# Hybrid attention and expert step on one core: the second row block of gathered rows turned with 80 rows for every expert, and scattered with 80 for the last one

## The chip, the cores and the metric

The kernel is one program on 1 core of a Trainium2 chip. The metric is the device time of one execution in microseconds (us); lower is better. The kernel of before has a median of 1916.29 us over 3 runs.

## What is computed

One inference step of a two-layer backbone with shared weights, for 128 context tokens and 512 latent tokens of width 1024, all in fp32. Each layer has a modulated RMSNorm, a mixer (differential attention beside a short convolution), a second RMSNorm and a SwiGLU channel mixer. The first layer's mixer is dense. The second layer's picks 2 of 8 experts for each token, and that is where the change lies:

```python
def moe_swiglu(h, w_router, w_gu, w_down):
    logits = (t @ w_router).astype(jnp.float32)
    top_v, top_i = lax.top_k(logits, TOP_K)
    top_w = jax.nn.softmax(top_v, axis=-1)
    gates = jnp.einsum('nk,nke->ne', top_w, jax.nn.one_hot(top_i, N_EXPERTS, ...))
    g, u = jnp.split(jnp.einsum('nd,edf->enf', t, w_gu), 2, axis=-1)
    eo = jnp.einsum('enf,efd->end', jax.nn.silu(g) * u, w_down)
    y = jnp.einsum('ne,end->nd', gates, eo)
```

The result is scaled by a gate, added to the residual stream, and normalized once more.

## The kernel before

**Engines and number format.** Tokens are columns, features are partitions, in most stages. Every fp32 weight tile of 128 x 1024 (a chunk) is loaded by the SP queue into one of 6 buffers `raw` (L604), rounded by ACT to `w_hi` (L1383), and DVE forms the rest `w_lo` (L1943), in 3 buffers. TensorE (PE) multiplies hi by hi, hi by lo and lo by hi. PSUM is one tensor `ps` of 4 slots, each of two banks of 512 columns. PE waits in `open_block` for a slot, and DVE frees slots by `blk_free`.

**The experts.** Where no expert has more than 208 tokens the kernel computes only the chosen rows. The experts are sorted by load. `ROOM` (L29) is the number of slots for each: 208, 192, 184, 176, 168, 160, 160, 160. Each expert's rows lie in two row blocks: the first has 128 rows, the second the rest. `NROWS` (L30) is `[128, ROOM - 128]` for each expert: second blocks of 80, 64, 56, 48, 40, 32, 32, 32 rows. `ROWS` (L28) is `[128, 80]`, the largest.

**Order of work.** `main_items` (L89) writes the order out by hand, and `main_plan` (L109) numbers the steps and gives each its PSUM slot. All engines follow the same list in `main_expert`. For each expert e it is: 22 chunks up (`gu`), then the two `tr` steps of expert e+1, then 11 chunks down (`down`). A chunk's split for two steps later is queued on ACT and DVE at the head of each step.

**Turning the rows.** GpSimd gathers the rows of an expert's tokens from memory into `gx` (L1829), `NROWS[e]` rows of each block, well ahead. A `tr` step (L1253 to L1261) transposes four feature blocks of `gx` into a PSUM slot, for each the first row block (128 rows) and then the second (`NROWS[e][1]` rows), so two steps make 16 transposes per expert. The pieces of feature block k lie at column `(k % 2) * ROOM[e]`, the second at 128 beyond. ACT copies the slot to `hg` (L1620) and DVE forms the low part (L2450), `2 * ROOM[e]` columns of each bank.

**The last expert.** The outputs of experts 0 to 6 go through memory and are joined to the residual `x_tok` while the last expert runs. The last one stays on the chip. For each half of 512 features and both row blocks DVE scales `ey` (L2485), ACT rounds it to `ey_hi` (L1631), and DVE makes `ey_lo` (L2495), `NROWS[7]` rows each, 128 and 32. PE then scatters the rows to the tokens by the selection `selT`. For tokens of tiles 0 and 1 the sum starts from `x_tok` (`seed`, L1195) and `scatter_on` (L1204) adds four matmuls for each half, waiting for each operand. They go in the order hi of block 0, hi of block 1, lo of block 0, lo of block 1. For tiles 2 to 4 `scatter` (L1131) does four matmuls for each half without waits, in the order hi and lo of block 0, hi and lo of block 1.

**The end.** For each tile of 128 tokens: DVE adds the scatter to `x_tok` (L2503, tiles 2 to 4), ACT squares and sums (L1653) and takes the root (L1656), DVE the reciprocal (L2521). ACT scales the row (L1636), or GpSimd for tiles 2 and 3 (L1898). PE turns it back (`turn_tokens`, L1220, with one dummy product L1214 before most). DVE (L2528) and ACT (L1804) multiply by the last gain, and SP stores ten blocks of 256 KB (L695).

Of the kernel before, what the change touches and what calls it, by code (L numbers as in the profile page):

```python
# [263 lines left out]
def hybrid_step(nc, xT, condT, ada_w, in_w, out_w, gu_w, down_w, router_w, b_ada, g_mix, g_ffn, g_fin, lam_qk,  # L264
                subln, conv_w, kcT, vc, cos, sin, ident, iota, below, moe_down_w, y, newk, newv):
    with ExitStack() as ctx:
# [494 lines left out]
        def _(pe):  # L761
# [115 lines left out]
            for l in range(LAYERS):  # L877
# [193 lines left out]
                else:  # L1071
# [51 lines left out]
                                     start=True, stop=True).then_inc(mm_done, 1)  # L1123
                    tile_rows(7, 4)

                    def scatter(g, t, hf, u, nrows=ROWS):

                        for st_ in range(ST):
                            rows = slice(0, nrows[st_])
                            for part in (ey_hi, ey_lo):  # L1130
                                ins = nc.tensor.matmul(ps[:, g % 4, hf, :], selT[rows, u, st_, t * P:(t + 1) * P],  # L1131
                                                       part[rows, st_, hf * 512:(hf + 1) * 512],
                                                       start=(st_ == 0 and part is ey_hi),
                                                       stop=(st_ == ST - 1 and part is ey_lo))
                        return ins
# [62 lines left out]
                    def scatter_on(g, t, hf, hi_count):  # L1198

                        for part, ready in ((ey_hi, ahi_done), (ey_lo, alo_done)):  # L1200
                            for st_ in range(ST):
                                rows = slice(0, NROWS[LAST_E][st_])
                                pe.wait_ge(ready, hi_count + st_ + 1)
                                ins = nc.tensor.matmul(ps[:, g % 4, hf, :], selT[rows, 1, st_, t * P:(t + 1) * P],  # L1204
                                                       part[rows, st_, hf * 512:(hf + 1) * 512], start=False,
                                                       stop=(st_ == ST - 1 and part is ey_lo))
                        return ins
# [22 lines left out]
                    def main_expert(part):  # L1230
                        oo = operand[l, "act"]
                        for kind, e, i, q, g, c in part:
# [11 lines left out]
                            if kind == "idx":  # L1244
                                fill(g0 + g + 1, FILL["ranks"])
                                pe.wait_ge(sel_ready, 1)
                                pe.wait_ge(tok_ready, 1)
                                for st_ in range(ST):
                                    for t in range(TT):
                                        ins = nc.tensor.matmul(ps[0:ROWS[st_], slot, st_, 0:2],  # L1250
                                                               sel[:, t, st_ * P:st_ * P + ROWS[st_]], tok[:, t, :],
                                                               start=(t == 0), stop=(t == TT - 1))
                            elif kind == "tr":  # L1253
                                if i == 0:
                                    pe.wait_ge(gx_in, 16 * ST * (e + 1))
                                for k in range(4):
                                    for st_ in range(ST):
                                        at, some = (k % 2) * ROOM[e] + st_ * P, NROWS[e][st_]
                                        ins = nc.tensor.transpose(ps[:, slot, k // 2, at:at + some],  # L1259
                                                                  gx[0:some, st_, (4 * i + k) * P:(4 * i + k + 1) * P],  # L1260
                                                                  idn[0:some, 0:some])  # L1261
                            elif kind == "gu":
                                if i == 0:
                                    if e == 0:
                                        fill(g0 + g, FILL["rows"])
                                    pe.wait_ge(alo_done, oo + LO_BASE[e] + 2)
                                ins = up_chunk(n0 + c, ps[:, slot, 0, 0:ROOM[e]], ps[:, slot, 0, 0:2 * ROOM[e]],
                                               gathered_rows(e))
                            elif kind == "turn":
                                pe.wait_ge(gates_ready, 1)  # L1270
                                pe.wait_ge(sel_ready, 2)
                                ins = turn_slots(slot, i, glast)
                            elif kind == "xt":
                                ins = turn_stream(slot, i)
                            else:
                                pe.wait_ge(alo_done, oo + LO_BASE[e] + 2 + i + 1)
                                if e == 0:
                                    ins = down_chunk(n0 + c, g0 + g, i)
                                elif (e, i) == (LAST_E, FB - 1):

                                    down_upper(n0 + c, g0 + g, i).then_inc(upper_done, 1)
                                    ins = down_lower(n0 + c, g0 + g, i)
                                else:
                                    down_lower(n0 + c, g0 + g, i)
                                    ins = down_upper(n0 + c, g0 + g, i)
# [67 lines left out]
                    with pe.Else():  # L1353
# [9 lines left out]
                        for t, hf in LAST_ORDER:  # L1363
                            if t in SEEDED:
                                scatter_on(lg + t, t, hf, last_lo - ST * (2 - hf)).then_inc(mm_done, 1)
                                if (t, hf) == (0, 0):
                                    seed(lg + 1, 1, 1)
                                continue
                            if hf == 0:
                                open_block(lg + t)  # L1370
                            scatter(lg + t, t, hf, 1, NROWS[LAST_E]).then_inc(mm_done, 1)
                        turn_tokens(lg + TT, POOLED, 1)


# [1 line left out]
        def _(act):  # L1376
# [75 lines left out]
            for l in range(LAYERS):  # L1452
# [142 lines left out]
                else:  # L1595
# [29 lines left out]
                    def last_outputs_hi():  # L1625
                        for hf in range(2):
                            for st_ in range(ST):

                                rows, cols = slice(0, NROWS[LAST_E][st_]), slice(512 * hf, 512 * (hf + 1))
                                act.wait_ge(ey_scaled, ST * hf + st_ + 1)  # L1630
                                nc.scalar.activation(ey_hi[rows, st_, cols], ey[rows, st_, cols], ACT.Copy)\  # L1631
                                    .then_inc(ahi_done, 1)
# [299 lines left out]
        def _(dve):  # L1932
# [138 lines left out]
            for l in range(LAYERS):  # L2071
# [246 lines left out]
                else:  # L2318
# [158 lines left out]
                    def last_outputs(g, done0):  # L2477
# [3 lines left out]
                        for hf in range(2):  # L2481
                            cols = slice(512 * hf, 512 * (hf + 1))
                            for st_ in range(ST):
                                rows = slice(0, NROWS[LAST_E][st_])
                                nc.vector.scalar_tensor_tensor(  # L2485
                                    ey[rows, st_, cols], ey[rows, 1, cols] if st_ else ps[rows, g % 4, hf, :],
                                    gslot[rows, 1, st_:st_ + 1],
# [2 lines left out]
                                dve.wait_ge(ey_scaled, 2 * ST)  # L2490
                                dve.sem_inc(blk_free, ST)
                            for st_ in range(ST):
                                rows = slice(0, NROWS[LAST_E][st_])
                                dve.wait_ge(ahi_done, done0 + ST * hf + st_ + 1)
                                nc.vector.tensor_tensor(ey_lo[rows, st_, cols], ey[rows, st_, cols],  # L2495
                                                        ey_hi[rows, st_, cols].bitcast(F32), ALU.subtract)\
# [375 lines left out]
```

## Time and profile before

| | |
|---|---|
| median of 3 runs | 1916.29 us (1916.16 to 1916.88) |
| the profiled execution | 1912.51 us |
| its span on the core | 1910.7 us |
| mean granted TensorE clock | 0.985 |
| PE, DVE, ACT, GpSimd busy | 97%, 58%, 41%, 7% of the span |
| expert stage, first turned row to last down matmul | about 1231.7 to 1872.3 us |
| from there to the end | 38.4 us |

The profile is one execution. PE is the matmul side of TensorE, PEld its weight loads, which run beside the matmuls; a transpose is recorded as one load and one matmul. A shape such as `32*128 32x32` reads: 32 active rows and 128 active columns of the array, operand of 32 partitions by 32 elements. Starts of matmuls are recorded, their ends are modelled, so the distance from start to start tells the pace, and "busy" does not show gaps between pipelined instructions. "Idle ... <-issue" is time in which an engine waited for nothing that the profile shows. The granted clock is the share of TensorE's full 2.4 GHz that it was allowed.

### The profile page before, as it was taken

The page shows a single profiled execution, that of the slowest core. Times are in us where ns is not written, and L with a number is a line of the kernel's source. Part 1 is how long each engine was busy: PE and PEld are TensorE (multiplying, and loading weights), DVE is VectorE, ACT ScalarE, POOL GpSimd, SP SyncE. Part 2 cuts the span into 40 slices and gives each one's busy share as a digit, 9 for nine tenths or more (in the row PEclk, how much of TensorE's full clock was granted, in tenths as well). Part 3 has the DMA queues.
Part 4 walks back from the last instruction along what each step waited for, and adds up shares of the span by engine and source line. Part 5 has one row for each costly group of instructions (what it writes and reads, how often), then busy time and mean ns, then how long its engine had stood idle before and what let it go on. Part 6 is the DMA issues. An engine that isn't in the chain of part 4 may idle for free.

```text
span 1910.7 us, 30889 instructions
## 1 busy us (share of the span) xinstructions
PE 1844.9 (97%) x12347; PEld 1690.1 (88%) x12347; DVE 1115.5 (58%) x1907; ACT 790.8 (41%) x1335; POOL 142.7 (7%) x109
## 2 busy tenths in 40 slices
PE   7999989999999999999999899699999999999988
PEld 6999867999999999999998579697998989989875
DVE  2653786453432344447437862575776867768685
ACT  4221264422221222232222643364655656656564
POOL 2000000200000000020000001330000000002211
PEclk8999999999999999999999999799999999999997
DMA  9425100323332242223363000596787877878861
GB/s 359 171 101 221 56 1 12 122 100 140 115 100 78 100 179 86 78 89 142 123 191 86 1 15 9 157 233 206 226 285 218 266 234 241 272 223 328 271 192 56
DMA packets 93847, 290.56 MB, mean 152 GB/s; under 512 B 15368, under 2 KB 23944, under 8 KB 93696
## 3 DMA queue, kind: packets, MB, share of 16 engines
q1 hardware_dynamic: 86784, 271.20, 43.4%
q0 software_dynamic: 6912, 17.30, 2.7%
q8 instruction: 101, 1.65, 0.4%
q14 instruction: 50, 0.41, 0.1%
HBM read 281.98 MB, written 12.28 MB: 154 GB/s over the span
## 4 chain that ended last, share of the span: by engine, by line
PE 88%; DVE 5%; issue 2%; ACT 2%; DMA 1%; POOL 0%; SPq 0%; ACTq 0%; DVEq 0%; POOLq 0%
PE ps L776 48%; PE ps L1144 11%; PE ps L1167 6%; PE ps L1145 5%; PE ps L1177 4%; PE ps L842 2%; PE ps L971 2%; PE ps L917 2%; PE ps L1155 2%; PE ps L1148 2%; PE ps L1259 1%; DVE nbias L2099 1%; PE ps L1147 1%; DVE pr L2116 1%; PE ps L1131 1%
## 5 line engine op out<-in xcount | busy, mean ns | idle before, releaser
L1943 DVE TENSOR_TENSOR w_lo<-raw,w_hi 128x1024 fp32r<-128x1024 f32 x394 | 482.6, 1225 | 354.8 <-ACT w_hi L1383 345.4
L1383 ACT ACTIVATE w_hi<-raw 128x1024 fp32r<-128x1024 f32 x394 | 414.5, 1053 | 320.8 <-PE ps L776 171.1
L1144 PE MATMUL ps<-hg,w_hi 128*128 128x320 f32 (+5 forms) x1232 | 348.0, 352 | 6.3 <-DVE w_lo L1943 4.0
L776 PE MATMUL ps<-a_hi,w_hi 128*128 128x320 f32 x1472 | 341.4, 313 | 3.4 <-DVE a_lo L1974 3.4
L776 PE MATMUL ps<-a_hi,w_lo 128*128 128x320 f32 x1472 | 336.5, 310 | 0.0
L776 PE MATMUL ps<-a_lo,w_hi 128*128 128x320 f32 x1472 | 333.4, 307 | 0.0
L1145 PE MATMUL ps<-hg,w_lo 128*128 128x160 f32 (+5 forms) x1232 | 301.5, 245 | 0.0
L776 PEld LDWEIGHTS ps<-a_hi,w_hi 128*128 128x128 f32 x1472 | 247.0, 188 | 12.1 <-issue 8.1
L776 PEld LDWEIGHTS ps<-a_lo,w_hi 128*128 128x128 f32 x1472 | 248.4, 188 | 0.0
L776 PEld LDWEIGHTS ps<-a_hi,w_lo 128*128 128x128 f32 x1472 | 245.0, 188 | 0.0
L1144 PEld LDWEIGHTS ps<-hg,w_hi 128*128 128x128 f32 x1232 | 233.6, 190 | 7.9 <-DVE w_lo L1943 4.5
L1145 PEld LDWEIGHTS ps<-hg,w_lo 128*128 128x128 f32 x1232 | 236.7, 192 | 0.4
L1991 DVE TENSOR_REDUCE bcol<-ps 128x2 f32<-128x4 f32 x84 | 13.5, 160 | 184.9 <-PE ps L776 184.8
L1167 PE MATMUL ps<-w_hi,ea 128*128 128x512 f32 x308 | 85.9, 401 | 3.6 <-DVE w_lo L1943 3.6
L776 PE MATMUL ps<-act_hi,w_hi 128*128 128x320 f32 x352 | 80.3, 309 | 0.0
L776 PE MATMUL ps<-act_hi,w_lo 128*128 128x320 f32 x352 | 80.3, 309 | 0.0
L776 PE MATMUL ps<-act_lo,w_hi 128*128 128x320 f32 x352 | 80.3, 309 | 0.0
L1911 POOL COPY ss<-sq 128x640 f32<-128x640 f32 x4 | 3.3, 822 | 1022.9 <-ACT sq L1394 1022.9
L917 PE MATMUL ps<-kT,qT 64*128 64x512 f32 (+2 forms) x288 | 63.4, 486 | 11.9 <-ACT pr L1501 11.9
L1594 ACT ACTIVATE act_hi<-tt 128x640 fp32r<-128x640 f32 x22 | 16.3, 740 | 140.9 <-DVE tt L2000 140.9
L1501 ACT ACTIVATE pr<-ps,nbias 128x768 f32<-128x768 f32 (+1 forms) x80 | 63.5, 794 | 26.6 <-DVE nbias L2099 15.3
L1167 PEld LDWEIGHTS ps<-w_hi,ea 128*128 128x128 f32 x308 | 57.6, 189 | 17.4 <-DVE w_lo L1943 4.3
(321 smaller groups left out, 2633.7 us busy)
## 6 DMA issues: line engine op xcount, KB each, us to landing
raw<-gu_w SPq DMA_DIRECT2D x220, 512.0 KB
raw<-moe_down_w SPq DMA_DIRECT2D x88, 512.0 KB
ada_raw<-ada_w SPq DMA_DIRECT2D x21, 2048.0 KB, 8.1
raw<-in_w SPq DMA_DIRECT2D x48, 512.0 KB
raw<-down_w SPq DMA_DIRECT2D x22, 512.0 KB
raw<-out_w SPq DMA_DIRECT2D x16, 512.0 KB
ada_pro<-ada_w SPq DMA_DIRECT2D x2, 2048.0 KB, 18.9
y_rows<-ey POOLq DMA_DIRECT2D x7, 512.0 KB
```

The costliest lines, as they stand in the source:

```text
L776: ins = nc.tensor.matmul(out[:, hf, 0:c1 - c0], w, o[:, c0:c1], start=f, stop=e)
L842: ins = nc.tensor.matmul(ps[32 * j:32 * (j + 1), g % 4, 0, 0:QCOLS], cs[:, QUAD * q + k, :], src[:, k, j * QCOLS:(j + 1) * QCOLS], start=f ...
L917: ins = nc.tensor.matmul(score_rows(l, m)[:, c0:c1], qT[rows, h, t * P:(t + 1) * P], kT[rows, h, k0 + c0:k0 + c1], start=True, stop=True)
L971: ins = nc.tensor.matmul(outputs(l)[:, i % 2, :], pT[:, i % 2, j * P:(j + 1) * P], vtok[:, k0 // P + j, h * VH:(h + 1) * VH], start=(j == ...
L1144: nc.tensor.matmul(sums, whi, both, start=(k == 0), stop=False)
L1145: nc.tensor.matmul(out, wlo, rows_[:, k, 0, :], start=False, stop=False)
L1148: ins = nc.tensor.matmul(sums, whi, both, start=False, stop=True)
L1167: ins = nc.tensor.matmul(ps[:, g % 4, hf, :], ea[:, k, LOWER * a:LOWER * a + P], w[:, n % SPLIT, hf * 512:(hf + 1) * 512], start=(k == 0 a ...
L1177: ins = nc.tensor.matmul(ps[:, (g + 1) % 4, hf, :], ea[:, k, P:2 * P], w[:, n % SPLIT, hf * 512:(hf + 1) * 512], start=(k == 0 and w is w_ ...
L1383: nc.scalar.activation(w_hi[:, s, :], raw[:, n % RAW, :], ACT.Copy).then_inc(hi_done, 1)
L1501: nc.scalar.activation(pr[:, i % 2, s, 0:nk], score_rows(l, m)[:, 0:nk], ACT.Exp, bias=nbias[:, m % 4:m % 4 + 1], accum_out=rsum[:, STEPS[ ...
L1943: nc.vector.tensor_tensor(w_lo[:, s, :], raw[:, n % RAW, :], w_hi[:, s, :].bitcast(F32), ALU.subtract)\
```

## The change

Everywhere that `NROWS` limited the second row block on PE or in the last expert's operands, `ROWS` takes its place: 80 rows for every expert. The gather (L1828) and the copies of outputs (L2656, L2667, L1734) keep `NROWS`. The rows of `gx` above those gathered hold what an earlier expert left there; their columns in PSUM are overwritten by the next transpose or lie outside what is copied. In the scatter the added slots have zeros in `selT`.

```diff
@@ scatter, and its call for the last expert
-                    def scatter(g, t, hf, u, nrows=ROWS):
+                    def scatter(g, t, hf, u):
-                            rows = slice(0, nrows[st_])
+                            rows = slice(0, ROWS[st_])
...
-                            scatter(lg + t, t, hf, 1, NROWS[LAST_E]).then_inc(mm_done, 1)
+                            scatter(lg + t, t, hf, 1).then_inc(mm_done, 1)
@@ scatter_on
-                                rows = slice(0, NROWS[LAST_E][st_])
+                                rows = slice(0, ROWS[st_])
@@ main_expert on PE, kind == "tr"
-                                        at, some = (k % 2) * ROOM[e] + st_ * P, NROWS[e][st_]
+                                        at, some = (k % 2) * ROOM[e] + st_ * P, ROWS[st_]
@@ last_outputs_hi on ACT
-                                rows, cols = slice(0, NROWS[LAST_E][st_]), slice(512 * hf, 512 * (hf + 1))
+                                rows, cols = slice(0, ROWS[st_]), slice(512 * hf, 512 * (hf + 1))
@@ last_outputs on DVE, at L2484 and at L2493
-                                rows = slice(0, NROWS[LAST_E][st_])
+                                rows = slice(0, ROWS[st_])
```

## Rows read from the trace of the kernel before

**Rows 1.** The page, part 1 (PE) and part 4 (chain that ended last).
```profile
PE 1844.9 (97%) x12347; PEld 1690.1 (88%) x12347; DVE 1115.5 (58%) x1907; ACT 790.8 (41%) x1335; POOL 142.7 (7%) x109
...
PE 88%; DVE 5%; issue 2%; ACT 2%; DMA 1%; POOL 0%; SPq 0%; ACTq 0%; DVEq 0%; POOLq 0%
```

**Rows 2.** Timeline of PE, expert 0's transposes: start us, us, engine, line, operands, count.
```profile
1232.32 1.16 PE L1259 MATMUL ps<-idn,gx 80*128 80x80 f32 x11
1233.32 0.31 PE L809 MATMUL ps<-ones 128*128 128x128 f32 x1
```

**Rows 3.** Stretches, L1259 alone: us, PE busy, PEld busy, clock, DMA share, GB/s.
```profile
1291.97:1295.60 3.63, 3.63 (x16) 2.04 (x15) 1.00 0.72 244
...
1532.92:1536.40 3.48, 3.48 (x16) 2.05 (x15) 1.00 0.83 247
...
1762.39:1765.80 3.41, 3.41 (x16) 2.05 (x16) 1.00 0.98 315
```

**Rows 4.** Groups by shape, L1259's weight loads: busy, mean ns | idle before.
```profile
L1259 PEld LDWEIGHTS ps<-idn,gx 32*128 32x128 f32 x24 | 3.2, 134 | 3.1 <-issue 0.6
...
L1259 PEld LDWEIGHTS ps<-idn,gx 80*128 80x128 f32 x7 | 1.0, 142 | 0.0
```

**Rows 5.** Timeline of PE, the last down chunks (eight starts between the two).
```profile
1868.62 0.63 PE L1167 MATMUL ps<-w_lo,ea 128*128 128x512 f32 x2
...
1870.49 0.63 PE L1177 MATMUL ps<-w_lo,ea 128*128 128x512 f32 x2
```

**Rows 6.** The chain that ended last, in order of time: start us, us, what.
```profile
1878.46 4.94 PE ps L1204 x12
1883.40 13.32 PE ps L1131 x24
```

**Rows 7.** Stretches of the tail: PE, PEld, DVE, ACT, POOL busy, clock, DMA.
```profile
1882.00:1884.00 2.00, 2.00 (x6) 0.84 (x5) 0.16 (x1) 1.70 (x4) 0.00 (x0) 0.98 0.00 0
1886.00:1890.00 4.00, 4.00 (x8) 1.74 (x8) 1.39 (x2) 1.15 (x3) 0.00 (x0) 0.50 0.00 0
1894.00:1898.00 4.00, 4.00 (x12) 2.35 (x12) 1.22 (x1) 0.86 (x3) 2.54 (x1) 0.50 0.00 0
1898.00:1902.00 4.00, 4.00 (x25) 4.00 (x25) 2.82 (x6) 2.60 (x4) 2.84 (x1) 0.63 0.41 118
```

**Rows 8.** Timeline of DVE beside expert 7's transposes.
```profile
1763.26 0.31 DVE L2629 TENSOR_TENSOR tt<-tt,ps 128x160 f32<-128x160 f32 x1
...
1767.61 1.23 DVE L1943 TENSOR_TENSOR w_lo<-raw,w_hi 128x1024 fp32r<-128x1024 f32 x1
```

**Rows 9.** Groups by shape on DVE, the last expert's scaling: busy, mean ns.
```profile
L2485 DVE SCALAR_TENSOR_TENSOR ey<-ps,gslot,x 128x512 f32<-128x512 f32 x2 | 1.5, 740 | 0.0
L2485 DVE SCALAR_TENSOR_TENSOR ey<-ey,gslot,x 32x512 f32<-32x512 f32 x2 | 1.5, 730 | 0.0
```

**Rows 10.** Timeline of the end on DVE, ACT and POOL.
```profile
1896.76 1.22 DVE L2503 TENSOR_TENSOR x_tok<-x_tok,ps 128x1024 f32<-128x1024 f32 x1 [3.18 <-PE ps L1131]
1898.02 1.06 ACT L1653 ACTIVATE yab<-x_tok 128x1024 f32<-128x1024 f32 x1 [3.12 <-DVE x_tok L2503]
1898.13 0.16 DVE L2521 RECIPROCAL trms<-trms 128x1 f32<-128x1 f32 x1
1898.38 2.84 POOL L1898 TENSOR_SCALAR yab<-x_tok,trms 128x1024 f32<-128x1024 f32 x1 [1.84 <-DVE trms L2521]
...
1900.29 1.15 ACT L1636 ACTIVATE yab<-x_tok,trms 128x1024 f32<-128x1024 f32 x1 [0.80 <-DVE trms L2521]
1903.16 2.24 ACT L1804 ACTIVATE x<-ps,gfin 128x128 f32<-128x128 f32 x8 [1.72 <-PE ps L1220]
```

**Rows 11.** Timeline of PE, one up chunk's first matmul and the next one's.
```profile
1758.27 0.31 PE L1144 MATMUL ps<-hg,w_hi 128*128 128x320 f32 x1
1758.42 0.23 PE L1145 MATMUL ps<-hg,w_lo 128*128 128x160 f32 x1
...
1760.33 0.31 PE L1144 MATMUL ps<-hg,w_hi 128*128 128x320 f32 x1
```

More of the change, by code:

```diff
@@ L2492, in last_outputs @@
                             for st_ in range(ST):
-                                rows = slice(0, NROWS[LAST_E][st_])
+                                rows = slice(0, ROWS[st_])
                                 dve.wait_ge(ahi_done, done0 + ST * hf + st_ + 1)
```

## Prediction

> **What bounds the kernel now.** I read the page's busy times and its chain first, then the timeline of TensorE (PE) where the diff touches it, then the weight loads' idle time, then the granted clock. PE is busy for 97% of the span and carries 88% of the chain that ended last [rows 1], so a microsecond taken off PE's own stream in the expert stage should come off the time, as long as ACT and DVE, which split the weights for it, keep up. "Busy" is no proof of useful work, though, and the timeline shows where. The sixteen transposes of expert 0 (second block 80 rows) run at 11 starts in 1.00 us, 0.091 us each [rows 2]. The same sixteen of experts 1 to 7 (second block 64, 56, 48, 40, 32, 32, 32 rows) take 3.63 us down to 3.41 us, 0.21 to 0.23 us each, at the full granted clock ([rows 3] hold experts 1, 4 and 7 of the seven). They move fewer columns and take over twice as long. The weight loads say why: of the 32-row loads each has about 0.13 us of idle before it (3.1 us over 24), while the 80-row loads of expert 0 have none [rows 4]. So a load for the full array is fetched ahead behind the running transpose, and one that changes from 128 rows to 64 or fewer, or back, waits until the array is empty. Expert 0 alternates 128 and 80 rows and pays nothing: 80 is on the side of 128.
>
> The Trainium skill fits these rows: its page "TensorEngine Tiling (Array Packing)", Key Properties, says that changing the tiling mode drains TensorE, and its Tiling Modes are 128, 64 or 32 rows; by that rule 80 rows need the undivided array, and the trace agrees ([rows 2, 3]).
>
> The last scatter has the same pattern, 128 rows and 32 rows in turn. A 128x512 matmul of the last down chunks starts every 0.234 us (8 in 1.87 us) [rows 5]. The seeded scatter (L1204) needs 4.94 us for 12, 0.41 each, and the plain one (L1131) 13.32 us for 24, 0.555 each [rows 6]. The second figure has another part: the granted clock is 1.00 until shortly before 1884, 0.50 from there to 1898, and is on its way back within 1898 to 1902 [rows 7]. That is 1.2 in place of 2.4 GHz. Before it fell PE had no idle time by the records, but it was streaming 512 columns only half of the time, half of them with 32 rows; it rose in the transposes that follow, all 128 rows and dense.
>
> **The change, part by part.**
>
> *Turned rows.* Seven experts have 16 transposes each, 8 of them widened to 80 rows. Today: 3.63 + 3.59 + 3.53 + 3.48 + 3.42 + 3.42 + 3.41 = 24.48 us [rows 3]. After: 7 x 16 x 0.091 = 10.2 us [rows 2]. That is 14.3 us less, the added columns included, because expert 0 already moves 80. The bounds: 14.3 less where the gap is wholly a matter of row count, and 1.8 more where it is not (rivals, below). I take the first, because expert 0 is the same line, tiles and queue.
>
> *What hides behind it.* Behind each block stand the down chunks of the expert before. They need the last up block out of PSUM (DVE L2629, ends 1763.57 for expert 7) and later w_lo of the third chunk (starts 1767.61, ends 1768.84) [rows 8]. PE comes to the first at 1762.39 + 1.46 = 1763.85, 0.3 us after it is free. It comes to the third chunk at 1763.85 + 20 x 0.234 = 1768.5. That is before 1768.84, but this split stands in ACT's and DVE's queues behind the second copy of the turned rows, which waits for PE today; with the turn 1.9 us earlier, the two copies run back to back and w_lo ends near 1768.0. What is late next is thus just in time; I give back 0.3 us over all seven blocks, with 0 and 7 us (1 us each) as ends.
>
> *Nothing else moves there.* The gathers still bring 64 to 32 rows; rows above stay what an earlier expert left and fall outside what is used. No DMA, wait or queue entry is added or moved. The copies out of PSUM keep their sizes.
>
> *Last expert on ACT and DVE.* Four copies and eight DVE operations go from 32 to 80 partitions at the same 512 columns. The 32-partition form takes 730 ns, the 128-partition one 740 [rows 9]: 0.1 us in all, taken as 0.
>
> *Seeded scatter.* The first four of its matmuls wait for ey_hi and ey_lo, as now. The other 12: 4.94 us today, 12 x 0.234 = 2.8 after [rows 5, 6]: 2.1 us less. No row shows waits of this kind without a change of rows; if the wait before each matmul also keeps its load back, the gain is 0. I take 2.1, since the idle time before the loads of [rows 4] comes with the row change alone, with no wait between those transposes.
>
> *Plain scatter.* 24 x 0.234 = 5.6 us at the full clock, against 13.32: 7.7 us less [rows 5, 6]. I take the full clock: the engine now has neither 32-row matmuls nor empty stretches, and the down chunks before, dense and of 128 rows, run at 2.4 GHz (512 columns are 0.213 us there, the start distance 0.234). At the low clock it is 24 x 0.47 = 11.2, only 2.1 less.
>
> *What is late next at the end.* The tail has a second chain: per token a DVE add of 1.22, ACT square 1.06 and two small steps (1.7 in all with the handoffs, an estimate), reciprocal 0.16, scaling about 1.1; for tokens 2 and 3 the scaling is on GpSimd at 2.84 [rows 10]. Run forward with these, in times that leave the turned rows' gain out: PE ends the seeded scatter near 1881.1, token 2 at 1882.9, token 3 at 1884.8, token 4 at 1886.6. ACT begins token 0 near 1880.3 and has it scaled at 1884.4; token 2, added by 1884.2, is squared and rooted by 1885.9, and only then token 1 is scaled, by 1886.9. That frees PSUM for the transposes, 0.3 us after PE is through. GpSimd scales token 2 from 1886.2 to 1889.1 and token 3 to 1892.0; the transposes of tokens 3 and 4, 1.1 us each, follow to 1894.3. Today they run to about 1904.2: the last ACT copies, which wait for them, end at 1905.40 [rows 10]. So the end comes 9.9 us earlier, and the stores behind it (the last ACT copy ends at 1905.40, the span at 1910.7) have a little more room. I take 10.0.
>
> **Sum.** 14.3 - 0.3 + 10.0 = 24.0 us. The profiled execution took 1912.51 us with a span of 1910.7, so 1.8 lie around it; it would be 1888.5. The median of the runs is 1916.29, 3.8 above the profiled one, and I keep that distance: **1892 us**.
>
> **Rivals.**
>
> 1. *The low clock stays in the scatter.* For it: the fall in the present tail starts right after the seeded scatter, whose waits on ACT and DVE remain. Against: [rows 7] show the full clock still in 1882 to 1884, more than 3 us into its last twelve matmuls, and those now come closer together. Gain 14.0 + 2.1 + 2.1 = 18.2: 1898. Chance 0.13.
> 2. *Waits take the place.* At each block the down chunks wait for w_lo or PSUM after all, 1 us per block; the tail gains. 24 - 7 = 17: 1899. For it: the 0.3 us of slack. Against: order and lengths of the copies. Chance 0.06.
> 3. *Only columns count.* The gap is something else than the rows, such as what happens to run beside experts 1 to 7. From 64 to 32 rows a block loses 0.22 us for 256 columns, 0.86 ns a column [rows 3]; the change adds 8 x (16+24+32+40+3x48) = 2048 columns: +1.8 us; the scatter keeps its 512 columns and changes by nothing: 1918. Against it: the pace is uniform in seven blocks, and the idle time goes with the row change [rows 4]. Chance 0.06. The Trainium skill's page "TensorE: Matmul & The Clock Gate", Step-by-step, says of a weight load that its time scales with the columns and that the row count does not matter: by it alone nothing would be gained; the loads' own lengths agree (134 ns at 32 rows, 142 at 80), the idle before them does not.
> 4. *Slower: writes in PSUM wait for each other.* The widened transpose writes columns 128 to 207, and the next one begins at column 192 to 160, over its last 16 to 48. That is 4 places per expert, 28 in all. If today's distances are waits for a former write to the same bank, they stay, and each overlap adds up to another 0.21 us: 28 x 0.21 + 1.8 = 7.7: 1924. With the distances kept, 0.07 us per place makes it slower by over 0.2%; were they gone, 0.9 us would be needed. Against it: the sixteen matmuls of an up chunk, 1758.27 to 1760.33, all write the same columns and start 0.13 us apart (2.06 us over 16), while they last 0.23 to 0.31 us and more [rows 11]. Chance 0.05.
>
> That the wider shape is not what runs can be left out: the line takes it from ROWS, as expert 0 does today.
>
> **How the numbers follow.** The likeliest case has 0.70, its own range 1889 to 1895 (distance of the runs to the profile, 0 to 3 us of waits, up to 2 us of the seeded scatter, 1 us of stores). The range to 1900 takes in rivals 1 and 2, and 1888 allows the stores to end sooner. Rivals 3 and 4 are left out, with 0.11. A measurement of this kernel tells some 0.2%, 3.8 us, from no change. Faster: 0.70 + 0.13 + 0.06 = 0.89; within 0.2%: rival 3, 0.06; slower: rival 4, 0.05.
>
> **What would show it.** Turned rows: seven blocks of 16 transposes near 1.5 us each, no idle before the 80-row loads. If PE's first down matmul is followed by idle with w_lo or PSUM named, rival 2 holds. Tail: L1131 in about 5.6 us at clock 1.00; near 11 at 0.50 is rival 1. GpSimd's second scaling should become the releaser of a wait on PE. Blocks of 3.5 us with 80 rows mean that rivals 3 or 4 hold and my reading of the gap is wrong; above 5 us it is rival 4.

## The result, and the profile after

| | before | after |
|---|---|---|
| median | 1916.59 us (4 runs, 1916.16 to 1920.43) | 1885.99 us (4 runs, 1884.07 to 1886.11) |
| profiled execution | 1912.51 us | 1886.11 us |
| its span | 1910.7 us | 1884.3 us |
| mean granted clock in it | 0.985 | 0.990 |

The ratio is 0.9839, 95% interval 0.982 to 0.9858 (27.2 to 34.5 us): 30.6 us faster by the medians, 26.4 us by the two profiled spans. The forecast was 1892 with a range of 1888 to 1900, so the kernel came out below the range.

The page of after, parts 1 and 4, against [rows 1]:

```profile
PE 1818.4 (97%) x12347; PEld 1680.9 (89%) x12347; DVE 1115.4 (59%) x1907; ACT 789.5 (42%) x1335; POOL 141.1 (7%) x109
...
PE 87%; DVE 6%; issue 2%; DMA 2%; ACT 2%; POOL 1%; SPq 0%; POOLq 0%; ACTq 0%; DVEq 0%
```

PE has the same 12347 instructions and is 26.5 us less busy. Its share stays at 97%: this was never idle time by the records, but matmuls that stood behind each other.

Stretches of the turned rows in after, L1259 alone (columns as in [rows 3]), and the groups of its weight loads by shape between 1286 and 1800 us, which answer to [rows 4]:

```profile
1290.18:1291.61 1.43, 1.43 (x16) 1.43 (x15) 1.00 0.74 264
1525.00:1526.43 1.43, 1.43 (x16) 1.43 (x15) 1.00 0.81 255
1748.56:1750.06 1.50, 1.50 (x16) 1.44 (x16) 1.00 0.99 366
```

```profile
L1259 PEld LDWEIGHTS ps<-idn,gx 80*128 80x128 f32 x56 | 8.0, 142 | 0.1
L1259 PEld LDWEIGHTS ps<-idn,gx 128*128 128x128 f32 x56 | 7.9, 142 | 0.0
```

The seven blocks take 1.43 to 1.54 us each, 10.3 in all where they took 24.4. The idle time before the narrow loads, 3.1 us over 24, is 0.1 over 56. The weight loads themselves became no shorter (142 ns, where the 32-row loads took 134): only the gaps between them went.

The chain that ended last in after, its last pieces in order of time (start us, us, what), which answers to [rows 6]:

```profile
1863.82 1.45 PE ps L1204 x5
1865.26 3.75 PE ps L1131 x16
1869.01 0.02 issue
1869.03 1.23 DVE x_tok L2503
1870.27 0.02 issue
1870.29 0.17 DVE trms L2521
1870.46 0.09 issue
1870.56 2.86 POOL yab L1898
1873.42 2.83 POOLq L266
1876.25 0.04 issue
1876.30 1.11 PE ps L1220 x8
1877.40 0.02 issue
1877.43 1.46 ACT x L1804 x5
```

In before, PE carried this chain alone from the seeded scatter to the last transposes. Now it leaves PE after token tile 2 and runs through GpSimd's two scalings (2.86 and, under POOLq, 2.83 us) back to PE. The timeline of PE has the wait that the prediction asked for:

```profile
1876.30 1.09 PE L1220 MATMUL ps<-idn,yab 128*128 128x128 f32 x8 [1.51 <-POOL yab L1898]
```

The clock in the tail of after (columns as in [rows 7]) stays at 1.00 until PE has done its work:

```profile
1861.00:1863.00 2.00, 2.00 (x8) 1.31 (x7) 1.49 (x3) 1.26 (x2) 0.00 (x0) 1.00 0.00 0
1865.00:1868.00 3.00, 3.00 (x15) 2.43 (x14) 1.00 (x2) 2.94 (x7) 0.00 (x0) 1.00 0.01 3
1868.00:1871.00 3.00, 2.86 (x13) 1.99 (x11) 1.94 (x4) 2.67 (x6) 0.44 (x1) 1.00 0.02 5
```

Read between first starts of PE's lines, the spans differ so:

| stretch | before | after | gained |
|---|---|---|---|
| start to expert 1's block | 1291.97 | 1290.18 | 1.8 |
| the seven blocks | 24.4 | 10.3 | 14.2 |
| between the blocks, and down to the seeded scatter's first start (L1195) | 555.9 | 555.6 | 0.3 |
| L1195 to the plain scatter (L1131) | 10.98 | 9.02 | 2.0 |
| L1131 to the first final transpose (L1220) | 13.32 | 5.91 | 7.4 |
| L1220 to the end | 14.01 | 13.28 | 0.7 |

That is 26.4. (From the first start of L1204, the seeded scatter itself went from 7.93 to 5.80 us, 2.1 gained.) The other 4.2 of the 30.6 is the distance between median and profiled execution: +4.1 before (1916.59 against 1912.51), -0.1 after.

### The profile page after: what moved, and what is told of

Read it like the earlier page. It is cut to its first block, busy times and chain, and to the rows that moved or that the text cites. A ratio compares the mean times of both kernels' runs of the same rounds, so it can differ in the third digit from the quotient of the medians.

```text
span 1884.3 us, 30889 instructions
## 1 busy us (share of the span) xinstructions
PE 1818.4 (97%) x12347; PEld 1680.9 (89%) x12347; DVE 1115.4 (59%) x1907; ACT 789.5 (42%) x1335; POOL 141.1 (7%) x109
## 4 chain that ended last, share of the span: by engine, by line
PE 87%; DVE 6%; issue 2%; DMA 2%; ACT 2%; POOL 1%; SPq 0%; POOLq 0%; ACTq 0%; DVEq 0%
PE ps L776 48%; PE ps L1144 11%; PE ps L1167 5%; PE ps L1145 5%; PE ps L1177 4%; PE ps L842 3%; PE ps L971 2%; PE ps L917 2%; PE ps L1155 2%; PE ps L1148 2%; DVE nbias L2099 1%; PE ps L1147 1%; DVE pr L2116 1%; DVE w_lo L1943 1%; DMA yab<-y_rows,late 1%
## 5 line engine op out<-in xcount | busy, mean ns | idle before, releaser
L1144 PE MATMUL ps<-hg,w_hi 128*128 128x320 f32 (+5 forms) x1232 | 346.8, 351 | 5.0 <-DVE w_lo L1943 3.7
L1144 PEld LDWEIGHTS ps<-hg,w_hi 128*128 128x128 f32 x1232 | 232.9, 189 | 6.6 <-DVE w_lo L1943 4.2
L1167 PE MATMUL ps<-w_hi,ea 128*128 128x512 f32 x308 | 85.8, 401 | 3.7 <-DVE w_lo L1943 3.6
L1167 PEld LDWEIGHTS ps<-w_hi,ea 128*128 128x128 f32 x308 | 57.5, 189 | 17.7 <-DVE w_lo L1943 4.8
```

The costliest lines, as they stand in the source:

```text
L1144: nc.tensor.matmul(sums, whi, both, start=(k == 0), stop=False)
L1167: ins = nc.tensor.matmul(ps[:, g % 4, hf, :], ea[:, k, LOWER * a:LOWER * a + P], w[:, n % SPLIT, hf * 512:(hf + 1) * 512], start=(k == 0 a ...
```

## The experiments

Two things were open: whether the row change is the cause, and where its limit lies; and why the gain by medians is so much above the forecast. All ratios are to the kernel of before, run on the same chip beside them. Times between first starts are used throughout, so that seeded means first start of L1204 to first of L1131, and plain from there to the first of L1220 (before: 7.93 and 13.32; after: 5.80 and 5.91).

### Each part alone

**before_again** is the kernel of before unchanged.

> The kernel before, unchanged. Theory A: the change itself is worth 14.2 us in the turned rows and 10.1 in the tail; the rest of the difference of the medians (30.6 us) is how executions of the same code differ, by how long the low clock lasts around the start of the expert stage (1208 to 1242 us in the trace of before) and in the tail. It expects a median near 1916 here, and spans of single executions that differ by steps of 1.7 us or more, with the mean granted clock going with them; the profile of before was a short one. Rival B: the change also shortens a part outside the turned rows and the tail. It expects every execution here, profiled or not, within 0.5 us of the others in the stages up to the expert stage, and the profiled execution at 1912.5 again.

It has a median of 1915.69 us over 10 runs (1912.38 to 1918.22), ratio 0.9994 (0.998 to 1.0007). Its profile showed what that of before had not. Stretches of before_again over expert 1's block and right behind it (columns as in [rows 7]):

```profile
1290.70:1294.40 3.70, 3.70 (x18) 2.16 (x17) 2.65 (x6) 1.53 (x3) 0.00 (x0) 1.00 0.77 245
1294.40:1298.00 3.60, 3.60 (x11) 2.45 (x12) 2.33 (x3) 1.75 (x2) 0.00 (x0) 0.60 0.04 18
```

The clock falls as the turned rows end, for 3.4 us, here and again at 1380 behind expert 2's block. The stages with these falls are longer than the same stages of before: 86.28 against 84.71 us and 79.93 against 78.45. One fall costs some 1.5 to 1.6 us.

The tail differs too. The clock falls at 1882.2, inside the seeded scatter and 2.7 us before the plain one, and stays low for 20.5 us; in before it fell at 1883.9, just behind the plain one's start, for 17.1 us. The stretch between that fall and the plain scatter, then the two scatters in the chain:

```profile
1882.20:1884.80 2.60, 2.60 (x4) 0.91 (x4) 0.16 (x1) 1.39 (x3) 0.00 (x0) 0.50 0.00 0
```

```profile
1878.91 6.02 PE ps L1204 x12
1884.93 13.80 PE ps L1131 x24
```

So seeded takes 9.00 us and plain 13.80, and from the first start of L1204 to the end it is 36.8 us against 35.3 in before and 25.0 in after.

**turn_only** widens only the transposes:

```diff
-  at, some = (k % 2) * ROOM[e] + st_ * P, NROWS[e][st_]
+  at, some = (k % 2) * ROOM[e] + st_ * P, ROWS[st_]
```

> Only the transposes take 80 rows; the last expert's operands and scatter stay at 32. Theory A: seven blocks at 1.43 to 1.54 us in place of 3.4 to 3.6, the tail as before (10.98 us seeded, 13.32 plain), time 14 us below before: 1902. If the low clock in the tail depends on where the tail falls in time and not on what it does, the tail may be shorter: then 1892 to 1895. Rival that only columns count: 1.8 us above before.

1899.2 us (1894.84 to 1902.54), ratio 0.9903 (0.9874 to 0.9932). The blocks take 1.49 us; the tail is that of before_again (seeded 8.94 us, plain 13.80, at 0.50). By the medians the part is worth 17.7 us against before's 1916.89 beside it, where the blocks give 14.2; the interval (13.0 to 24.2 us) holds both. Behind expert 1's block the stretch of turn_only reads:

```profile
1294.40:1298.00 3.60, 3.60 (x17) 2.68 (x16) 2.81 (x4) 3.26 (x5) 0.00 (x0) 1.00 0.43 139
```

No fall behind any block. The chain:

```profile
1863.93 5.96 PE ps L1204 x12
1869.89 13.80 PE ps L1131 x24
```

**scatter_only** is after with the transposes set back to `NROWS[e][st_]` (the edit of turn_only the other way).

> Only the last expert's operands and scatter take 80 rows; the transposes keep 64 to 32. Theory A: transposes as before at 3.4 to 3.6 us a block; tail 10.1 us shorter, the seeded scatter's matmuls at 0.234 us where operands are there, the plain scatter 5.9 us at clock 1.00; time 1906. Rival: the clock falls here as in before, the plain scatter takes 11 us and the time is 1911.

1906.24 us (1905.15 to 1907.05), ratio 0.994 (0.9917 to 0.9963): worth 10.65 us. Seeded 5.79, plain 5.91 and end 13.27 are those of after to 0.01. The blocks are back at 3.4 to 3.8, and so are falls at their ends, at 1298 and 1462. The expected 1906 came, without the fall in the tail that its rival held possible.

**after_again** is the changed kernel once more.

> The changed kernel, unchanged, on the same chip as the three others. Theory A: 1886, the sum of the two parts within 1 us (before - turn_only plus before - scatter_only equals before - this). Rival B: the sum misses by 2 us or more.

1887.99 us (1886.8 to 1888.36), ratio 0.9844 (0.9822 to 0.9867), 28.9 below before's median; the parts alone sum to 17.7 + 10.65 = 28.3. No interaction shows, though the intervals are some 4 to 6 us to either side.

### Where the limit lies, and whether it is the changes or the width

**turn_64** and **turn_72** give every expert from 1 to 7 the same second row block in the transposes, in the kernel of before:

```diff
-  at, some = (k % 2) * ROOM[e] + st_ * P, NROWS[e][st_]
+  at, some = (k % 2) * ROOM[e] + st_ * P, (P, 64 if e else 80)[st_]
```

turn_72 has 72 in place of 64.

> The kernel before, with 64 rows in place of 56 to 32 in the second block's transposes of experts 2 to 7 (experts 0 and 1 as they are). Theory A (the array is emptied at each change between 128 rows and 64 or fewer): every block of experts 1 to 7 takes the 3.63 us of expert 1, idle before the loads stays, time some 0.9 us above before. Theory C, new after the first runs: behind such a block the granted clock falls to 0.50 for 3.4 us in some executions and costs 1.7 us each time; it expects such falls here as in before. Rival (fewer rows than 80 are slow by degrees): blocks of 2.5 us and less.

> The kernel before, with 72 rows in the transposes of experts 1 to 7. Theory A, by which 65 rows and more use the undivided array: blocks of 1.4 to 1.5 us, no idle before the loads, no fall of the clock behind them, time 1898 as with 80 rows alone (1899.2). Rival by degrees: blocks of 2 us and more.

turn_64: 1913.48 us (1910.2 to 1918.64, 10 runs), ratio 0.9991 (0.9977 to 1.0006), no difference that shows; its profile has the expected blocks, but none of the expected falls of the clock. turn_72: 1896.7 us (1896.33 to 1899.26), ratio 0.9897 (0.9875 to 0.992). A block of expert 5 in turn_64, the same view as [rows 3]:

```profile
1608.71:1612.34 3.63, 3.63 (x16) 2.06 (x16) 1.00 0.83 264
```

and the timeline of PE for expert 7's block in turn_72:

```profile
1748.96 1.58 PE L1259 MATMUL ps<-idn,gx 128*128 128x128 f32 x16
1750.46 0.70 PE L1167 MATMUL ps<-w_hi,ea 128*128 128x512 f32 x2
```

With 64 rows every block takes 3.63 us, with 72 it takes 1.38 to 1.50, with 80 it takes 1.43 to 1.54. The limit lies between 64 and 72 rows, and from 72 to 80 a block grows by some 0.05 us at most. This also explains the slope of [rows 3]: the fall from 3.63 to 3.41 us went with the size of the second row block (rows and columns shrink together in a transpose), since it is gone where the size is the same, and the rest of a block is the same sixteen gaps.

**turn_grouped** keeps the narrow rows of before and swaps the two loops, so that four blocks of 128 rows and then four narrow ones follow each other in each of the two steps: 4 changes of rows per expert in place of 16, and no matmul wider.

```diff
-  for k in range(4):
-      for st_ in range(ST):
+  for st_ in range(ST):
+      for k in range(4):
```

> The kernel before with its 64 to 32 rows, but each tr step transposes the four first row blocks and then the four second ones, so that the row mode changes 4 times per expert and not 16. Theory A (the change of mode costs, some 0.125 to 0.145 us each, not the small transpose): blocks of 1.8 to 2.0 us, time 1902 to 1904. Rival (transposes of 64 rows and fewer are slow in themselves, whatever stands beside them): blocks stay at 3.4 to 3.6, time 1916.

1903.26 us (1899.19 to 1908.66, 6 runs), ratio 0.9936 (0.9916 to 0.9955). The timeline of PE for expert 7's block:

```profile
1751.94 1.91 PE L1259 MATMUL ps<-idn,gx 128*128 128x128 f32 x16
1753.78 0.51 PE L1167 MATMUL ps<-w_hi,ea 128*128 128x512 f32 x1
```

1.84 us from start to start, against 3.41 with the same matmuls in turn: 1.57 us for 12 changes fewer, 0.13 us each. So it is the change of rows that costs, neither the narrow rows nor the columns. The seven blocks take 13.0 us in all; widening to 80 gains a further 2.7. This kernel's scatters are those of before, and slower still in its profile (seeded 12.94, low clock for 30.7 us from 1867), 4 us that go into its longest run, 1908.66; what made the clock fall earlier there is not known.

### The two scatters and the clock

**on_narrow** is after with only the seeded scatter back at 32 rows (`rows = slice(0, NROWS[LAST_E][st_])` at L1202). **plain_narrow** is after with only the plain scatter back (`scatter` takes `nrows` again, as in before):

```diff
-  scatter(lg + t, t, hf, 1).then_inc(mm_done, 1)
+  scatter(lg + t, t, hf, 1, NROWS[LAST_E]).then_inc(mm_done, 1)
```

> The changed kernel, but the seeded scatter (L1204) reads 32 rows of the second block again; the plain scatter keeps 80. Theory C: the seeded part takes 7.9 to 9.0 us again (2 to 3 more), and the clock, which falls for what is done in the seeded part, is at 0.50 as the plain scatter begins; with dense 128- and 80-row matmuls it comes back within the plain scatter, so that one takes 6 to 9 us. Time 1890 to 1893. Rival: the clock stays at 1.00 throughout, because only the plain part with 32 rows pulls it down: plain 5.9 us, 1890.

> The changed kernel, but the plain scatter (L1131) reads 32 rows of the second block again; the seeded one keeps 80. Theory C: the seeded part stays at 5.8 us; the plain one starts at clock 1.00, where its 24 matmuls are 0.335 us apart (8.0 us), and ends at 0.50 if the clock falls in it: 8 to 12 us against 5.9. Time 1889 to 1893. Rival: the clock never falls without the seeded part's gaps: 8.0 us and 1.00 to the end, 1889.

on_narrow: 1889.36 us (1888.6 to 1890.05), ratio 0.9861 (0.9839 to 0.9883); seeded 7.94, plain 6.01. Its chain, then its stretches over the scatter (columns as in [rows 7]):

```profile
1862.65 4.94 PE ps L1204 x12
1867.59 3.94 PE ps L1131 x16
```

```profile
1860.00:1867.00 7.00, 6.85 (x17) 2.87 (x16) 3.51 (x6) 2.53 (x5) 0.00 (x0) 1.00 0.00 1
1867.00:1873.00 6.00, 6.00 (x26) 4.64 (x25) 2.93 (x5) 4.76 (x10) 0.00 (x0) 1.00 0.01 4
```

Theory C expected a fall of the clock here, and it did not come: the narrow seeded scatter alone costs 2.1 us, all of it row changes.

plain_narrow: 1890.73 us (1890.1 to 1892.11), ratio 0.9869 (0.9847 to 0.9892); seeded 5.79, plain 7.82. Its chain and stretches:

```profile
1866.84 7.73 PE ps L1131 x24
```

```profile
1867.00:1874.00 7.00, 7.00 (x23) 3.12 (x22) 2.94 (x5) 5.87 (x11) 0.51 (x1) 1.00 0.02 4
1875.00:1879.00 4.00, 4.00 (x25) 4.00 (x24) 3.06 (x7) 2.40 (x4) 4.00 (x2) 0.62 0.23 64
```

The plain scatter with 32 rows takes 7.82 us at the full clock and 5.91 with 80: 1.9 us of row changes. The clock falls only behind it, for 3.4 us. So of the 7.4 us that plain gained in after, 5.5 (13.32 - 7.82) is clock and 1.9 is row changes, and in these profiles the clock is low in the plain scatter only where both scatters read 32 rows.

**scatter_64** is after with 64 rows in both scatters (`(P, 64)` at both places); ACT and DVE still make 80.

> The changed kernel, but both scatters read 64 rows of the second block: the mode changes as often as with 32, twice the rows are active. Theory A: seeded part 7.9 to 9.0 us, plain part at least 7.8. What lowers the clock in the tail of before is open: if it goes by the gaps that the mode changes leave, the clock falls here too, plain part 13.3 and more, time 1896 or above; if it goes by how many rows are active, it stays at 1.00 or comes back sooner, plain part 7.8 to 10, time 1891 to 1893.

1894.13 us (1889.65 to 1898.41), ratio 0.9893 (0.9863 to 0.9923). Its chain and stretches:

```profile
1865.81 4.95 PE ps L1204 x12
1870.76 5.31 PE ps L1131 x16
```

```profile
1863.00:1870.00 7.00, 6.84 (x17) 2.87 (x16) 3.67 (x6) 2.53 (x5) 0.00 (x0) 1.00 0.00 1
1870.00:1878.00 8.00, 8.00 (x25) 3.48 (x25) 2.94 (x5) 5.99 (x12) 0.38 (x1) 1.00 0.01 3
```

The pace is that of 32 rows (4.95 us for the twelve as in [rows 6]; plain 7.94 against 7.82), so in the scatter too 64 rows pay for the change in full. But the clock stays at 1.00 in this profile, where with 32 rows in both scatters it fell before or at the start of the plain one in all ten profiles that have them (plain 13.32 us in before, 13.80 in the other nine, where the fall came inside the seeded one). The same stretch in before_again:

```profile
1884.00:1898.00 14.00, 14.00 (x25) 6.27 (x25) 2.77 (x4) 6.30 (x11) 2.31 (x1) 0.50 0.01 2
```

It is one profile. The four runs spread over 9 us at mean clocks from 0.984 to 0.990, and their median lies above the 1891 to 1893 expected for a kept clock, so that 64 rows keep the clock in every execution isn't shown.

### What ends the kernel now

The new chain runs through GpSimd's scaling of tiles 2 and 3. **pooled_one** leaves it only tile 2 and gives tile 3 to ACT:

```diff
-SEEDED, POOLED, SHARED = (0, 1), (2, 3), (3, 4)
+SEEDED, POOLED, SHARED = (0, 1), (2,), (3, 4)
```

> The changed kernel with the scaling of token tile 3 on ACT and not on GpSimd, which is the releaser of PE's last wait in the trace of after (two scalings of 2.84 us in a row). Theory: the last transposes start 1.0 us sooner, time 1.0 us below after. Rival: ACT, which has the roots and the other scalings, is late in its place, no difference.

> The changed kernel once more, on the chip of the three others, to compare pooled_one with: 1886 to 1888.

pooled_one: 1887.68 us (1881.41 to 1891.19, 5 runs), ratio 0.9862 (0.9839 to 0.9885). **after_third**, the changed kernel beside it: 1885.37 us (1882.91 to 1889.58, 5 runs), ratio 0.9848 (0.9825 to 0.9872). The gain of 1.0 us did not come: L1220 to the end is 13.27 us in both. ACT ended 1.4 us sooner against the first transposes, but the ten stores had not. The stretch from 1865 to 1880 us in pooled_one, DMA busy tenths in 40 slices, and the stores:

```profile
DMA  1000000000008999999999999999999999995000
...
y<-x SPq DMA_DIRECT2D x10, 256.0 KB, 3.3
```

From the first store to the last the DMA engines are full: 2.62 MB at some 285 GB/s is 9.2 us. So the end goes with the start of the stores and what they take, not with the last scaling. pooled_one's own shortest execution (1881.41) is also the profiled one; its span is shorter ahead of the tail, not in it.

### More profiles of before

The falls behind the blocks could explain the excess of the medians, but the profile on which the forecast was made had none. **before_look1**, **before_look2** and **before_look3** are before unchanged, **turn_look1** is turn_only again, one profiled execution each.

> The kernel before, one more profiled execution. Theory C: in most executions of before the granted clock falls to 0.50 for 3.4 us right behind one to three of the seven blocks of turned rows of experts 1 to 7 (stage between two blocks 1.6 us longer each time). Rival D: the two falls seen in before_again and the two in scatter_only were chance, not tied to the blocks: falls then lie anywhere in the expert stage, or there are none.

> As before_look1: Theory C one to three falls, each right behind a block of turned rows; rival D none or elsewhere.

> As before_look1: Theory C one to three falls, each right behind a block of turned rows; rival D none or elsewhere.

> Only the transposes take 80 rows, one more profiled execution. Theory C: no fall behind any of the seven blocks. Rival D: as many as in before.

1909.68, 1910.54, 1917.84 and 1896.52 us, one run each; the one run of before beside them took 1923.12. The first two and turn_look1 have no fall behind a block. before_look3 has three, behind the blocks of experts 1, 4 and 7 (two stretches of block and what follows, then the third fall; columns as in [rows 7]):

```profile
1292.00:1295.70 3.70, 3.70 (x18) 2.13 (x16) 2.63 (x6) 1.53 (x3) 0.00 (x0) 1.00 0.81 248
1296.20:1299.50 3.30, 3.30 (x10) 2.30 (x9) 2.18 (x2) 1.27 (x2) 0.00 (x0) 0.55 0.01 2
1534.50:1538.00 3.50, 3.50 (x18) 2.09 (x16) 2.68 (x8) 1.29 (x3) 0.00 (x0) 1.00 0.78 247
1538.40:1541.50 3.10, 3.10 (x9) 2.39 (x8) 2.08 (x2) 1.34 (x2) 0.00 (x0) 0.50 0.06 24
1771.00:1773.00 2.00, 2.00 (x6) 1.60 (x5) 1.59 (x2) 1.18 (x2) 0.00 (x0) 0.50 0.71 289
```

Over all profiles of this case:

| turned rows | profiles | blocks | falls right behind a block |
|---|---|---|---|
| 64 to 32 rows, in turn (before, before_again, before_look1 to 3, scatter_only, turn_64) | 7 | 49 | 0, 2, 0, 0, 3, 2, 0: 7 |
| 72 or 80 rows, or grouped (the other eleven) | 11 | 77 | 0 |

Theory C's "in most executions" is not borne out: two of the five profiles of before have such falls. Nor are these the only falls of the stage. From expert 1's block to the seeded scatter the 18 profiles have 23 more, with narrow and with wide blocks alike, and each begins while PE waits 1.6 to 3.4 us for w_lo, or up to 1.8 us after that wait. Such a wait and the fall with it in before, a timeline line and a stretch with columns as in [rows 7]:

```profile
1740.09 0.41 PE L1144 MATMUL ps<-hg,w_hi 128*128 128x320 f32 x1 [2.32 <-DVE w_lo L1943]
```

```profile
1740.60:1744.00 3.40, 3.40 (x16) 3.40 (x16) 3.04 (x6) 1.44 (x5) 2.79 (x3) 0.50 0.69 257
```

The seven of the table have no such wait near them. They begin between 0.8 us before and 0.6 us after the end of a narrow block.

## Why the prediction was right in its mechanism and missed the time

**Turned rows: right.** 14.3 us less was forecast, 14.2 came, with gathers, ACT and DVE left as they were. At each change between 128 rows and 64 or fewer PE loses some 0.13 us; it is shown by changing the rows and nothing else (turn_64 against turn_72) and by changing the order and nothing else (turn_grouped).

**Rival 3 falls, rival 4 falls.** Columns cost some 0.8 ns each (a block of expert 1 takes 1.38 us in turn_72 and 1.43 in after, with 64 columns more), near the 0.86 of [rows 3], but the change did not come out slower. The page "TensorE: Matmul & The Clock Gate" of the Trainium skill, Step-by-step, says that the row count does not matter to a weight load. For the load itself this holds (142 ns at 80 and at 128 rows, 134 at 32). For the pace of matmuls in turn it does not: turn_64 and turn_72 differ by 2.1 to 2.2 us per block. The widened transposes overlap a former one in PSUM at 28 places, and the blocks run at 0.09 us per transpose all the same, so writes to the same bank do not wait for each other here.

**Waits behind the blocks (0.3 us lost, rival 2 with 7): right that they are small.** The stretch between the blocks came out 0.3 us shorter in this pair, but it differs by more between profiles of one kernel (before 552.5 to 558.5 us, after 552.6 to 555.7), so 0.3 either way can't be read from it. That rival 2 is out is shown by the waits: PE's waits of the expert stage in after name w_lo alone, 3.7 us in front of L1144 and 3.6 in front of L1167, two each; before they were 4.0 and 3.6.

**Seeded scatter, 2.1 us: right** for the row changes (2.1 in the first pair, 2.1 in on_narrow). The waits before each of its matmuls do not keep the loads back: where the operands are there, starts are 0.23 to 0.24 us apart. In the four other profiles of before the clock falls inside this scatter, which then takes 8.7 to 9.0 us, so that 2.9 to 3.2 are gained; the sum had no term for that.

**Plain scatter, 7.7 us at the full clock: right** (7.4 measured, 5.91 against 5.6; 7.9 against the 13.80 of the four other profiles). Rival 1, the low clock staying, is dead: in all seven profiles with 80 rows in one scatter or both, the clock is 1.00 through it. The reason given was partly wrong. "Neither 32-row matmuls nor empty stretches" named two things, and scatter_64, with the gaps and without the 32 rows, kept the clock too. By that one profile the active rows counted, not the gaps alone.

**End, in all 10.0 us for the tail: right for this pair** (10.1), with GpSimd's second scaling as the releaser. That it fits so well is in part luck of the profile: from the first start of L1204 to the end, before's first profile took 35.3 us, its four others 36.5 to 36.8, and after 25.0 each time, so 11.5 to 11.8 is what the tail gains in those. That ACT's and DVE's wider operands cost next to nothing holds too: the scaling L2485 of block 1 takes 739 ns with 80 partitions, 730 with 32. But the 0.7 us behind L1220 is bounded by the stores, not by GpSimd, as pooled_one shows.

**The sum against the profiled pair.** It gave 24.0 us, and 26.4 came. Of the difference 1.8 lies ahead of expert 1, where nothing changed. The low clock at the start of the expert stage lasted 20.5 us in before and 17.1 in after, and between 13.7 and 23.9 in other executions of either kernel. That is chance of the execution.

**The step that failed** in the prediction is "the median of the runs is 1916.29, 3.8 above the profiled one, and I keep that distance". It takes the distance for something that lies around both kernels alike. It did not stay: it was 4.1 us before and -0.1 after. Part of it is time that this change takes away, and that the one profile of before, from which every term was read, happened not to have:

- Falls of the clock behind narrow blocks: none in that profile, 0, 2, 0, 0 and 3 in the five of before, so one per execution on the mean, 1.6 us. The sum had no term for the clock there, because the one profile showed 1.00 in all seven blocks.
- The earlier fall in the tail: 1.2 to 1.5 us in the four other profiles, 1.1 on the mean of the five.

With both, the sum is 24.0 + 1.6 + 1.1 = 26.7. By the means of the profiles the stretches that the change touches gain 27.2 us: 14.2 in the blocks, 1.6 in the falls behind them, 11.4 from L1204 to the end. Without the distance kept, the sum as it stood gives 1912.5 - 24.0 = 1888.5, above the 1886.0 that was measured (1888.0 and 1885.4 for the same kernel later).

**What stays open.** These terms narrow the gap and don't close it. 1916.29 less 26.7 is 1889.6, and the medians of after lie 28.9 to 30.6 us below those of before beside them. The means of the whole profiled executions lie 25.0 apart (1913.0 for the five of before, 1888.0 for the three of after), 2.2 less than those 27.2. Of the 2.2, 1.7 us is the stretch ahead of expert 1, the same code in every kernel, which took 1288.8 to 1294.3 us in the 18 profiles and happened to be short in before's. The median of before is 1915.6 to 1916.9 in every batch with several runs, 2.6 to 3.9 us above the mean of its profiled executions; that of after is 0 to 2.6 below the mean of its own. The granted clock points the same way: in the 13 runs of before beside the first batch it is 0.977 to 0.984, mostly 0.981, while its five profiled executions have 0.981 to 0.986. But six of those runs have the same 0.981 and differ by 5 us (1914.57 to 1919.63), so it is not the clock alone. Executions of before without a profile may have more falls; where in them the clock was low is not recorded, so this isn't shown.

No kernel tried was faster than after; pooled_one and after_third can't be told apart.

## What to carry to other kernels

Matmuls of alternating row counts are worth a look where one of them is at 64 rows or fewer: signs are starts further apart than the columns explain, and weight loads with idle time named "issue" before them just where the rows change. Either take them all well above 64 rows (72 and 80 were measured), even if the added rows are empty, or sort them so that equal rows stand together; four changes in place of sixteen gave back 11.4 of the 14.2 us. And take the profiled execution for what it is, one draw: where the clock falls in some executions and not in others, read two or three profiles, for the size of each term as much as for the distance to the median, and ask which part of that distance lies in the stretches that the change takes away.

## What the runs showed of the hardware that was not expected

- The limit of the row modes, seen through their cost: 72 and 80 rows stand beside 128 without a gap, 64, 56, 48, 40 and 32 do not. A change costs 0.12 to 0.14 us in the transposes at the full clock, and 0.16 in the plain scatter (1.9 us over its 12 changes).
- The clock can fall to 0.50 for 3.4 us at the end of a block of 16 transposes that took 3.4 to 3.8 us, though PE is "busy" all the while by the records. It costs the dense down chunks that follow 1.5 to 1.6 us. It came in 7 of 49 such blocks, and in none of 77 that took 1.4 to 1.9 us.
- With both scatters at 32 rows in turn with 128 the clock was low in the plain one in all ten profiles, with both at 64 rows and the same pace it was not in the one profile there is: 13.32 to 13.80 against 7.94 us for the same 24 matmuls. With only one of the two at 32 rows it stayed at 1.00 through both.
- The other falls of the expert stage, 23 in 18 profiles, each lie at a wait of PE of 1.6 to 3.4 us. Of the 39 waits of that length, 16 have no fall.
